# First norm of a two-block model taken on rows of tokens, in two halves, and the first two projection strips multiplied by halves

## The reference

```python
def rmsnorm(x, w):
    xf = x.astype(jnp.float32)
    xf = xf * lax.rsqrt(jnp.mean(xf * xf, axis=-1, keepdims=True) + EPS)
    return xf.astype(x.dtype) * w

def first_block(x, ...):
    cos, sin = rope_tables(positions, x.dtype)
    u = rmsnorm(x, norm_mix_w[l])
    proj = u @ w_in[l] + b_in[l]
    cb, cc, cx, q, k, v, g_conv, g_attn = jnp.split(proj, IN_SPLITS, axis=-1)
    q = apply_rope(q.reshape(...), cos, sin)
    k = apply_rope(k.reshape(...), cos, sin)
    ...
    x = x + merged @ w_mix_out[l]
    ...
```

## Time and profile before

| | us |
|---|---|
| median of 3 runs | 1891.19 |
| lowest and highest | 1889.92, 1892.54 |
| the profiled execution | 1891.45 |
| its span | 1889.7 |
| mean granted clock of TensorE in it | 0.988 of full |

### The profile page before, as it was taken

One profiled execution on the slowest core, in us unless ns is written; L12 is line 12 of the kernel. 1 busy time (PEld: TensorE's weight loads), 2 busy tenths in 40 slices (PEclk: granted clock), 3 DMA queues, 4 the chain that ended last, 5 costly groups with the idle time before them and its releaser, 6 DMA issues.

```text
span 1889.7 us, 20842 instructions
## 1 busy us (share of the span) xinstructions
PE 1851.8 (98%) x8613; PEld 1543.7 (82%) x8613; DVE 983.7 (52%) x1335; ACT 682.3 (36%) x1017; POOL 38.1 (2%) x72
## 2 busy tenths in 40 slices
PE   6899999999999999999999999999999999999998
PEld 5688888887888888888888888888888778888887
DVE  5555554457776766773333333657667453333332
ACT  5344442234332322343222222455566242222222
POOL 0000000000000000000000000101200000000001
PEclk9999999999999999979999999999999999999999
DMA  3222223354676665613333332322121223333333
GB/s 114 75 78 79 79 81 92 95 149 119 204 220 178 199 204 174 205 41 105 96 101 96 94 101 85 83 56 56 45 56 45 78 78 101 91 100 101 91 93 95
DMA packets 321716, 200.03 MB, mean 106 GB/s; under 512 B 6696, under 2 KB 311126, under 8 KB 321622
## 3 DMA queue, kind: packets, MB, share of 16 engines
q1 hardware_dynamic: 320128, 196.17, 35.7%
q0 software_dynamic: 640, 2.10, 0.4%
q10 hardware_dynamic: 854, 0.43, 0.1%
HBM read 196.57 MB, written 2.10 MB: 105 GB/s over the span
## 4 chain that ended last, share of the span: by engine, by line
PE 88%; DVE 4%; ACT 3%; DMA 3%; issue 1%; SPq 0%; POOL 0%; DVEq 0%; ACTq 0%
PE ps L1292 87%; DMA w_raw<-in_w_ffn_up 2%; PE ps L1295 1%; ACT w_hi L367 1%; DMA w_raw<-in_w_ffn_down 1%; DVE mod_acc L843 0%; DMA x_in<-in_x 0%; DVE t_b L814 0%; DVE w_lo L781 0%; DVE t_b L1019 0%; ACT t_b L403 0%; ACT y_hi L552 0%; DVE u_lo L802 0%; DVE x L825 0%; DVE ssum L792 0%
## 5 line engine op out<-in xcount | busy, mean ns | idle before, releaser
L1292 PE MATMUL ps<-u_hi,w_hi 128*128 128x512 f32 x1688 | 668.4, 396 | 8.6 <-DVE u_lo L802 3.3
L1292 PE MATMUL ps<-u_lo,w_hi 128*128 128x512 f32 x1688 | 660.7, 391 | 0.0
L1292 PE MATMUL ps<-u_hi,w_lo 128*128 128x512 f32 x1688 | 660.7, 391 | 0.0
L781 DVE TENSOR_TENSOR w_lo<-w_raw,w_hi 128x1024 fp32r<-128x1024 f32 (+2 forms) x307 | 364.5, 1188 | 285.7 <-ACT w_hi L367 284.9
L367 ACT ACTIVATE w_hi<-w_raw 128x1024 fp32r<-128x1024 f32 (+2 forms) x307 | 314.4, 1025 | 236.4 <-DMA w_raw<-in_w_down 77.8
L1292 PEld LDWEIGHTS ps<-u_hi,w_hi 128*128 128x128 f32 x1688 | 319.4, 189 | 80.4 <-issue 10.4
L1292 PEld LDWEIGHTS ps<-u_hi,w_lo 128*128 128x128 f32 x1688 | 319.0, 189 | 67.3
L1292 PEld LDWEIGHTS ps<-u_lo,w_hi 128*128 128x128 f32 x1688 | 319.4, 189 | 66.8 <-issue 2.4
L1292 PE MATMUL ps<-y_hi,w_hi 128*128 128x512 f32 x656 | 255.9, 390 | 0.7 <-DVE y_lo L1021 0.7
L1292 PE MATMUL ps<-y_hi,w_lo 128*128 128x512 f32 x656 | 255.3, 389 | 0.0
L1292 PE MATMUL ps<-y_lo,w_hi 128*128 128x512 f32 x656 | 255.2, 389 | 0.0
(11 more groups left out here) (255 smaller groups left out, 1434.8 us busy)
## 6 DMA issues: line engine op xcount, KB each, us to landing
mod_raw<-in_w_mod SPq DMA_DIRECT2D x72, 512.0 KB, 4.3
w_raw<-in_w_in SPq DMA_DIRECT2D x71, 512.0 KB, 3.9
w_raw<-in_w_ffn_up SPq DMA_DIRECT2D x44, 512.0 KB, 4.9
w_raw<-in_w_gate SPq DMA_DIRECT2D x44, 512.0 KB, 3.8
w_raw<-in_w_up SPq DMA_DIRECT2D x44, 512.0 KB, 3.8
w_raw<-in_w_down SPq DMA_DIRECT2D x32, 512.0 KB, 3.7
w_raw<-in_w_ffn_down SPq DMA_DIRECT2D x16, 512.0 KB, 5.8
w_raw<-in_w_down SPq DMA_DIRECT2D x16, 384.0 KB, 3.4
```

The lines of the kernel that those rows point to most:

```text
L781: e.tensor_tensor(w_lo[u % SLOTS][:, 0:n_k, :], w_raw[u % SLOTS][:, 0:n_k, :], f32(w_hi[u % SLOTS][:, 0:n_k, :]), ALU.subtract).then_inc(l ...
L1292: return e.matmul(out_, lhsT, rhs, start=start, stop=stop, skip_group_check=skip)
```

## The change

The first norm no longer works on transposed tiles. For each block tb of 128 tokens (a row of a token lies in one partition), ScalarE squares and sums the row as soon as the block has landed and takes Ln and Exp of the one column (row_norm), VectorE multiplies the row by it into x_norm (scale_row), and TensorE turns x_norm. The gain is applied in the eviction: ScalarE writes u_hi, VectorE u_lo, straight from PSUM (first_hi, first_lo), for 256 tokens at a time: half 0 is blocks 0 and 1, half 1 blocks 2 and 3. Five banks serve the turned halves in rotation. The first two strips are multiplied by halves, in the order strip 0 half 0, strip 1 half 0, strip 0 half 1, strip 1 half 1 (half_strip), with the turns of half 1 among them.

Other moves: sync loads identity and frequencies (129 columns) first, then two blocks of x, strip 0, block 2, strip 1, block 3, the rest of the constants, strips 2 and 3, and then the small vectors of the second and third tile, which scalar issued before. Plain x is turned behind rotations 0 to 3, two tiles each, and evicted by scalar behind q tiles 0 to 3. The angles stand behind the cuts of four strips in vector, their Sin behind the first eviction of q in scalar. The sum of squares by total, rstd and the 80 filler matmuls of the first norm are gone; 20 and twice 8 short ones (128 columns, warm_up) are new.

```diff
 def sync(e):
-            e.dma_start(consts[:, :], d["consts"]).then_inc(const_in, 16)
-            for tb in range(TB):
-                e.dma_start(x_in[:, tb, :], x_tok[:, tb, :]).then_inc(x_landed, 16)
+            e.dma_start(consts[:, 0:N_FIRST], d["consts"][:, 0:N_FIRST]).then_inc(first_in, 16)
+            load_x(0)
+            load_x(1)
+            load_strip(0)
+            load_x(2)
+            load_strip(1)
+            load_x(3)
+            e.dma_start(consts[:, C_ROT:N_CONST], d["consts"][:, C_ROT:N_CONST]).then_inc(const_in, 16)
+            load_strip(2)
+            load_strip(3)
+            for t in range(1, len(VEC_TILES)):
+                load_vec(e, t)
...
 def scalar(e):
+            def row_norm(tb):
+                e.wait_ge(x_landed[tb], 16)
+                after_own(e.activation(x_norm[:, tb, :], x_in[:, tb, :], ACT.Square, accum_out=ssq[:, tb:tb + 1]))
+                after_own(e.activation(row_r[:, tb:tb + 1], ssq[:, tb:tb + 1], ACT.Ln, bias=EPS_COL[EPS1], scale=1.0 / D_MODEL))
+                e.activation(row_r[:, tb:tb + 1], row_r[:, tb:tb + 1], ACT.Exp, scale=-0.5).then_inc(row_root, 1)
+            def first_hi(h, c):
+                e.wait_ge(half_turned, h * KC + c + 1)
+                e.activation(u_hi[:, c, half(h)], half_bank(h, c), ACT.Copy, scale=GAIN["mix"](c)).then_inc(half_hi if h == 0 else u_hi_set, 1)
...
-            norm("mix", 0)
-            for n in range(2):
-                e.wait_ge(angle_set, n + 1)
-                table = (sin_t, cos_t)[n]
-                e.activation(table, table, ACT.Sin).then_inc(tables_set, 1)
             for c in range(6):
...
+                if c == 1:
+                    for n in range(2):
+                        e.wait_ge(angle_set, n + 1)
+                        table = (sin_t, cos_t)[n]
+                        e.activation(table, table, ACT.Sin).then_inc(tables_set, 1)
                 e.activation(dst, ubank(u), ACT.Identity, bias=vcol("b_in", IN1["q"] // P + c)).then_inc(bank_read[u % 2], 1)
+                if c < 4:
+                    for v in (2 * c, 2 * c + 1):
+                        e.wait_ge(x_turned, v + 1)
+                        e.activation(x[:, v, :], bank(2 + v % 2), ACT.Copy).then_inc(x_set, 1)
...
 def vector(e):
+            def scale_row(tb):
+                e.wait_ge(row_root, tb + 1)
+                e.tensor_scalar(x_norm[:, tb, :], x_in[:, tb, :], row_r[:, tb:tb + 1], None, ALU.mult).then_inc(row_scaled, 1)
+            def first_lo(h, c):
+                e.wait_ge(half_hi if h == 0 else u_hi_set, c + 1)
+                e.scalar_tensor_tensor(out=u_lo[:, c, half(h)], in0=half_bank(h, c), scalar=GAIN["mix"](c), in1=f32(u_hi[:, c, half(h)]),
+                                       op0=ALU.mult, op1=ALU.subtract).then_inc(half_lo if h == 0 else u_lo_set, 1)
...
 def tensor(e):
-            keep_busy(40)
-            total("mix")
-            keep_busy(40)
+            for tb in range(2):
+                e.wait_ge(row_scaled, tb + 1)
+                for c in range(TURN_BANKS):
+                    turn_half(tb, c)
+                warm_up(8)
+            for k in range(KC):
+                half_strip(0, 0, k)
+                if TURN_BANKS + k < KC:
+                    turn_half(0, TURN_BANKS + k)
+                    turn_half(1, TURN_BANKS + k)
+            for k in range(KC):
+                half_strip(1, 0, k)
+                if k in (1, 5):
+                    tb = 2 + k // 5
+                    e.wait_ge(row_scaled, tb + 1)
+                    for c in range(TURN_BANKS):
+                        turn_half(tb, c)
...
-            unit_pair(U["qkv"], u_act, (u_lo_set, FILL["mix"] * KC))
             for c in range(1, 6):
                 if c > 1:
                     unit(U["qkv"] + c, u_act)
-                if c:
-                    rotate(c - 1)
+                rotate(c - 1)
+                if c < 5:
+                    for v in (2 * c - 2, 2 * c - 1):
+                        e.wait_ge(x_set, max(v - 1, 0))
+                        for tb in range(TB):
+                            ins = turn(ps[:, 2 + v % 2, tb * P:(tb + 1) * P], x_in[:, tb, v * P:(v + 1) * P])
+                        ins.then_inc(x_turned, 1)
```

More of the change, by code:

```diff
@@ L416, in scalar @@
+            for c in range(5, KC):
+                first_hi(0, c)
+            cut_hi(1)
+            row_norm(3)
             for c in range(KC):
-                e.wait_ge(x_turned, c + 1)
-                e.activation(x[:, c, :], bank(2 + c % 4), ACT.Copy).then_inc(x_set, 1)
-            squares("mix", lambda c: e.wait_ge(x_set, c + 1))
+                first_hi(1, c)
+            cut_hi(2)
+            cut_hi(3)
             e.wait_ge(vec_set, 3)
             e.activation(c_act[:, :], vec[:, VEC["c_2"]:VEC["c_2"] + KC], ACT.Silu).then_inc(silu_c_set, 1)
-            cut_hi(0)
@@ L795, in norm @@
                 f = FILL[which]
-                order = [FILL[n] for n in ("mix", "ffn0", "ffn1", "mix2", "ffn2")].index(f)
+                order = [FILL[n] for n in ("ffn0", "ffn1", "mix2", "ffn2")].index(f)
                 n0 = order * KC
@@ new lines, in half_strip @@
+            def half_strip(u, h, k):
+                if k == 0 and h == 0:
+                    e.wait_ge(lo_cut, u + 1)
+                e.wait_ge(half_lo if h == 0 else u_lo_set, k + 1)
+                ins = three(ubank(u)[:, half(h)], (w_hi[u][:, k, :], w_lo[u][:, k, :]), (u_hi[:, k, half(h)], u_lo[:, k, half(h)]), k == 0, k == KC - 1)
+                if k == KC - 1 and h == 1:
+                    ins.then_inc(unit_done, 1)
+            e.wait_ge(warm_set, 1)
+            warm_up(20)
+            e.wait_ge(first_in, 16)
@@ L1358, in rotate @@
+            for k in range(KC):
+                half_strip(1, 1, k)
             def rotate(c):
```

171 lines of the change are left out of this document (112 added, 59 removed).

## The result

The changed kernel takes 1881.20 us in the median of 4 runs (1880.54 to 1883.77), beside 1890.56 us for the kernel before. The ratio is 0.995, with a 95% interval of 0.9937 to 0.9964: 9.4 us faster where 17.6 were forecast, and 1.2 us above the range. The profiled execution took 1880.93 us, with a span of 1879.2 us and a mean granted clock of 0.989.

The account below looks back on a forecast made before the run. TensorE, busy 98% of the span, was taken as the bound, with only idle and half-clock stretches to win. Fifth rotation 38.5 + 3 x 7.29 + 1.7 = 62.1 for 79.66: gain 17.6, so 1873.85 us; range 1868.5 to 1880.

Parts of the forecast that it names:

- Everything behind 79.66: All work after the fifth rotation (of k) starts at 79.66 us; claimed untouched, so moving that mark gives the gain, 17.6 us.
- A: Rival: quicker front, no clock loss, gain 21.1 us, chance 0.25; in the profile's split, VectorE's low cuts 77 to 140.
- First product at 12.3: TensorE's first product matmul, on strip 0, starts at 12.3 us, 21 us ahead of before.
- rival B: Rival: slow front, gain 10 to 15 us, chance 0.23; in the profile's split, B is VectorE's low cuts 140 to 149.
- Strip 1 from 17.7: TensorE starts the products of strip 1 at 17.7 us, after VectorE's low cut ends at 17.6.
- angles ended at 37.2: VectorE's angles, behind the cuts of four strips, take 7.9 us and end at 37.2 us.
- TensorE idles 2.5 us ahead of rotation 1, at 38.5: TensorE waits 2.5 us for the eviction of q1, behind the Sin; the second rotation starts at 38.5 us.
- The charge of 1.7 us for the clock: Behind the idle time before the second rotation, 3.4 us at half clock, charged as 1.7 us.
- Periods of 7.29 us: The three periods from second to fifth rotation take 7.29 us each: 6.35 before plus 0.94 for eight turns of x.
- C: Rival: the start moves but the end doesn't, as another wait takes its place; within 0.2%, chance 0.04.
- D: Rival: the clock stays at 1.2 GHz through the whole projection; 8 us slower, about 1899 us, chance 0.03.
- 2 us to spare: Small vector loads, moved to SyncE's queue, land by 21 to 23 us; TensorE asks for them at 25.2.

Follow-up runs that it names:

- e0: The kernel before, unchanged, measured and profiled once more: 1890.26 us.
- after: The changed kernel as first measured and profiled: 1881.20 us.
- e11: The changed kernel with Sin behind the second eviction of q, without the twice 8 short fillers, plus 16 tiny matmuls ahead of the first rotation: 1878.82 us.
- h1: The kernel before with 34 more filler matmuls just behind its first feed-forward part: 1891.66 us.
- e7: The kernel before with the small vector loads moved to SyncE's queue behind the first four strips: 1895.24 us.
- e1: The changed kernel, unchanged, measured and profiled once more: 1878.16 us.
- g1: The changed kernel with 34 short fillers fewer, giving 8613 TensorE instructions as in the kernel before: 1875.15 us.
- e2: The changed kernel with the two Sin behind the second eviction of q instead of ahead of it: 1874.80 us.

## Why the prediction was wrong

- **"Everything behind 79.66 is not touched by the diff, so the change is worth what it moves that mark."** This is the step that failed, and it holds 5.4 of the missing 7.1 us. The code was not touched, its instructions' place in TensorE's stream was, and the clock did not stay out of it either. By the profile's own split: A is 3.2 us longer than before, which goes with the 34 instructions; B is the same as in that profile (1.6 longer than in e0); and 2.1 us more went behind B, where the kernel was at half clock once more, from 1225 to 1229 us. Behind B the half clock adds up to 13.7 us in after, e11 and h1, and to 10.2 us in the others (6.8 in e7), so this third part goes with neither kernel nor with the number. e1 did not have it, and its measurement, 1878.16 us, lies inside the range: that the first one came out 1.2 us above it is partly chance. With the number of instructions as before, g1's profiled execution took 1873.57 us where the prediction said 1873.85; that this is so close is luck, since g1 has other fillers and kept the clock that I had charged.
- **First product at 12.3, measured 13.70.** Two terms are in it. Strip 0 was there at 10.05 us for 9.5, and VectorE cuts it ahead of the low halves, so that the first of these ended at 12.8 instead of 12.25. TensorE then took the product only 0.9 us later, since it still had fillers to run that I had costed at nothing: block 1, scaled at 9.83, was turned from 11.02 behind the first 8, and the second 8 ran from 11.96 to 13.9, both for 1.95 us, at the slow pace. Block 0 was half a us late too (Square at 5.74 for 5.2), but ScalarE had 1.00 us to spare behind it. The slow pace was in rival B, and it came for half of strip 0: the 256-column matmuls start 0.21 us apart up to 17.1 us and 0.12 us from there.
- **Strip 1 from 17.7, measured 19.95; turns of block 3 at 20.6, measured 22.75; angles ended at 37.2, measured 39.06.** The later first product and the slow pace of strip 0 run through the chain: strip 1 started 6.2 us behind the first product, in e2, at full pace, 4.9. The terms themselves held: a row norm 1.7 us (5.74 to 7.44), low halves 2.04 us for five (0.41 each; I had 0.45), the angles 7.9 us (31.19 to 39.06), c_act 1.30 us behind the start of its table load. The traces have two table loads up to the mark where there were four, not three and five as I had counted. My end of strip 1 at 28.5 should have read 28.2 by its own terms; the sum did not use it.
- **TensorE idles 2.5 us ahead of rotation 1, at 38.5.** It idled 2.17 us, and the rotation came 1.3 us behind the angles (40.35), as said. The charge of 1.7 us for the clock was due in this execution (8.98 - 7.20 = 1.8), in others not: the row that I had taken it from was one execution.
- **Periods of 7.29 us, fifth rotation at 62.1.** 7.20, and 63.74. The front was off by 1.6 us; its gain of 15.9 us lies between my 17.6 and rival B's 10 to 15.
- **Rivals.** Of A, the low halves came true (0.41 us) and, in half of the executions, the clock, but strip 0 landed later than my figure and not earlier. B was right in the slow pace and its 1878 us is what e1 measured, but not by its way: its loss was to lie in the front. C and D did not come true. The vectors' queue, "2 us to spare", was right: no wait for them in the changed kernel.

## What to carry to other kernels

An edit in one stage shifts later instruction fetches, and where the DMA engines are full a fetch seems to hold up a strip: here 34 filler matmuls at the start were worth about 3 us (1.1 to 4.3), 400 us further on. Before a gain or loss of some 0.2% is put down to an edit's own work, compare stage by stage the part that was not touched, and try the edit with its instruction count evened out by fillers. And it can pay to move a wait for a late table (here Sin) behind one more eviction than the sum says: it was worth 2.3 us of the front here, and the clock besides where that was lost.

## What the hardware did that was not expected

- One instruction packet of 16 KB kept a DMA engine busy for about 1.1 us (1.1% of 16 engines over 6.3 us). With the engines 97% busy, the 78th cut came 0.8 to 1.5 us late in all eight executions in which a packet began 3.9 to 6.0 us ahead of it, and in none of the twelve others.
- The same idle time of 2.15 to 2.17 us was followed by a fall of the clock to 1.2 GHz in three of six executions and left it at 2.4 GHz in the other three.
- In the first 17 us of the changed kernel the pace of matmuls was half (0.21 us for 256 columns, against 0.12), and yet the window from 13 to 17 us reads a granted clock of 1.00. The trace's record of the clock begins only at 17.02 us there, just where the pace doubles (at 11.85 us in e2); ahead of its first entry the column shows 1.00 whatever the pace.
- A float32 matmul counts as two instructions: 68 in the program are 136 on the page.
